# Scan steps of a hybrid token mixer: reordered operations, running maxima computed ahead, and context tiles summed in one state

## What is computed

```python
# SSD, chunks of 128 tokens, per head: a = dt * A
states = einsum('bcqgn,bgrcq,bcqgrp->bcgrpn', Bc, exp(a_cum[..., -1:] - a_cum), xc)
y_diag = einsum('bcqgn,bcsgn,bgrcqs,bcsgrp->bcqgrp', Cc, Bc, exp(segsum(ac)), xc)
y_off = einsum('bcqgn,bcgrpn,bgrcq->bcqgrp', Cc, start_states, exp(a_cum))
# mLSTM, chunks of 128 tokens, per head: b = cumsum(logf)
g = b_last[..., None] - b + ic
m_loc = max(g, axis=-1)
w = exp(g - m_loc[..., None])
C_loc = einsum('bhcs,bcshd,bcshe->bchde', w, vc, kc)
def step(carry, inp):
    C, n, m = carry
    Cl, nl, ml, bl = inp
    m_new = maximum(bl + m, ml)
    C_new = exp(bl + m - m_new) * C + exp(ml - m_new) * Cl
    return (C_new, n_new, m_new), (C, n, m)
# then, with m0 the m before the chunk
m_t = maximum(b + m0, max(Dm, axis=-1)); s = (q @ k.T) * exp(Dm - m_t)
num = s @ v + (q @ C0) * exp(b + m0 - m_t); h = num / max(|den|, exp(-m_t))
```

## Time and profile before

| | |
|---|---|
| median of 3 runs | 3796.38 us (3788.16 to 3798.47) |
| profiled execution, its own time | 3790.32 us |
| its span | 3788.5 us |
| busy: TensorE, VectorE, ScalarE | 3603.6 (95%), 2733.1 (72%), 2024.5 us (53%) |
| attention, layer 0 and layer 1 | 250.0 to 292.1 and 2649.0 to 2672.0 us |
| scan on VectorE, layer 0 and layer 1 | 292.8 to 435.1 and 2672.9 to 2751.9 us |

### The profile page before, as it was taken

How to read it: one execution, slowest core, us unless ns; L and a number is a source line. 1 busy time by engine, 2 the same in 40 slices (tenths; PEclk the granted TensorE clock), 3 DMA queues, 4 the chain that set the end, 5 groups by cost and what they waited for, 6 DMA issues and landing times.

```text
span 3788.5 us, 61038 instructions
## 1 busy us (share of the span) xinstructions
PE 3603.6 (95%) x22630; PEld 3150.5 (83%) x22630; DVE 2733.1 (72%) x5634; ACT 2024.5 (53%) x4207; POOL 0.2 (0%) x4
## 2 busy tenths in 40 slices
PE   7999999999998999999999999989899999979998
PEld 5887787788887899999997888868698888868887
DVE  4556744499969688888768766674765899687666
ACT  3353522466668555555557544444454666684443
POOL 0000000000000000000000000000000000000000
PEclk9998899999999999999999999999999999999999
DMA  5213222356554566665665566533044565605665
GB/s 201 85 61 110 86 96 99 112 179 186 183 161 145 161 185 187 184 186 184 185 187 152 160 188 189 182 118 111 1 151 134 175 187 182 186 22 158 190 190 161
DMA packets 142198, 568.34 MB, mean 150 GB/s; under 512 B 15808, under 2 KB 17344, under 8 KB 130240
## 3 DMA queue, kind: packets, MB, share of 16 engines
q1 hardware_dynamic: 142016, 566.16, 47.5%
HBM read 565.05 MB, written 1.05 MB: 149 GB/s over the span
## 4 chain that ended last, share of the span: by engine, by line
PE 78%; DVE 17%; ACT 3%; issue 1%; DMA 0%; SPq 0%; DVEq 0%; ACTq 0%
PE ps L538 48%; PE ps L964 12%; PE ps L982 10%; DVE arena L1651 8%; PE ps L966 6%; DVE low L1651 3%; ACT arena L1133 2%; DVE hot_found L1651 1%; DVE arena L2143 1%; DVE arena L2134 0%; DVE ring_low L1651 0%; DVE arena L2136 0%; DVE arena L2131 0%; DVE arena L2140 0%; PE ps L752 0%
## 5 line engine op out<-in xcount | busy, mean ns | idle before, releaser
L1133 ACT ACTIVATE high<-ring 128x512 fp32r<-128x512 f32 x1632 | 1028.3, 632 | 1019.2 <-PE ps L538 499.1
L1651 DVE TENSOR_TENSOR low<-ring,high 128x512 fp32r<-128x512 f32 x1632 | 1075.5, 688 | 288.6 <-ACT high L1133 278.0
L538 PE MATMUL ps<-h_pair,high 128*128 128x512 f32 x3456 | 1234.7, 397 | 17.3 <-DVE h_pair L1651 10.1
L538 PE MATMUL ps<-h_pair,low 128*128 128x256 f32 x3456 | 978.6, 283 | 0.0
L538 PEld LDWEIGHTS ps<-h_pair,high 128*128 128x128 f32 x3456 | 652.5, 189 | 170.6 <-issue 11.9
L964 PE MATMUL ps<-wt,high 128*128 128x512 f32 x2048 | 713.2, 394 | 5.7 <-DVE low L1651 5.7
L538 PEld LDWEIGHTS ps<-h_pair,low 128*128 128x128 f32 x3456 | 653.8, 189 | 0.0
L966 PE MATMUL ps<-wt,low 128*128 128x256 f32 x2048 | 572.0, 279 | 0.0
L1133 ACT ACTIVATE arena<-ps 128x256 f32<-128x256 f32 (+2 forms) x658 | 273.3, 425 | 395.7 <-PE ps L538 348.1
L964 PEld LDWEIGHTS ps<-wt,high 128*128 128x128 f32 x2048 | 385.1, 188 | 93.0 <-issue 3.0
L538 PE MATMUL ps<-arena 128*128 128x128 f32 (+7 forms) x2536 | 373.2, 321 | 92.1 <-ACT arena L1133 64.4
(11 more groups left out here) (177 smaller groups left out, 4090.7 us busy)
## 6 DMA issues: line engine op xcount, KB each, us to landing
ring<-u_in SPq DMA_DIRECT2D x384, 512.0 KB, 3.6
ring<-v_in SPq DMA_DIRECT2D x384, 512.0 KB, 3.6
ring<-win_in SPq DMA_DIRECT2D x56, 1024.0 KB, 4.8
ring<-wmod_in SPq DMA_DIRECT2D x24, 1024.0 KB, 5.1
ring<-wq_in SPq DMA_DIRECT2D x48, 512.0 KB, 3.6
ring<-wmod_in SPq DMA_DIRECT2D x48, 512.0 KB, 3.8
ring<-wbr_in SPq DMA_DIRECT2D x16, 768.0 KB, 4.3
ring<-wout_in SPq DMA_DIRECT2D x8, 1024.0 KB, 4.9
```

The lines of the kernel that those rows point to most:

```text
L538: return pe.matmul(o, l_, r, start=first, stop=last)
L1133: return act.activation(o, i_, f, **kw_)
L1651: return dve.tensor_tensor(o, a, b, op)
```

## The change

It does four things. (1) In both layers the running maxima of all steps (`m_at`, `m_max`) and the weights `ap_` and `wk` (`carry`) are made at once, amid attention: two small matmuls turn `rr` and spread its maxima, VectorE runs `chain()` at entry 1, ScalarE one Exp. The steps then only read them. (2) In layer 0 the three blocks of rows of a step come from turned columns (`row_T`, made amid attention) with 32 rows of the array each, the three interleaved; the rows of a step stand ahead of its C·B products in both layers. (3) Within a step, VectorE makes `cb` and `xc` behind the small vectors and `rW` ahead of `ssd_m`; TensorE has the second modulation row and `ml_wT` ahead of `ssd_y`; `ml_num` is read ahead of `ml_dst`. (4) In layer 1 the two context steps of each direction are gone; `context_weights`, `context_states` and `context_read` make their summed state amid attention (entries 3 to 11), the decay of the first tile through the second folded into its weights.

```diff
+                pe.wait_ge(*at("decays", "cm", l))
+                b = claim("cums", "turn", l)
+                mm(b[0:32, 0:P], rr.rearrange("p a b -> p (a b)"), ident).then_inc(*inc("cums", "turn", l))
                 token_slot(s0 + SLOT_MV[1], "mv", 1, list(range(NT)))
+                b = claim("cums", "max", l)
+                pe.wait_ge(*at("decays", "diag", l))
+                mm(b[:, 0:32], ones[0:32, :], top_diag).then_inc(*inc("cums", "max", l))
...
+                def context_states(d):
...
+                    pe.wait_ge(*at("ml_kw", l, d, 1))
+                    pe.wait_ge(*at("ssd_xd", l, d, 1))
...
+                        for n in range(2):
+                            i = mm(b[gp, 0:256], B_tm[:, ORDER[d][n], gp], xd_ctx[n][:, g * 256:(g + 1) * 256],
+                                   n == 0, n == 1)
...
+                            for n in range(2):
+                                i = mm(b[:, (h % 2) * 129:(h % 2) * 129 + 129], kw_ctx[n][:, h * P:(h + 1) * P],
+                                       mv[:, ORDER[d][n], h, :], n == 0, n == 1)
...
+                    if s_ in (4, 8) and unshown(l):
+                        context_states(s_ // 4 - 1)
+                    if s_ == 8 and l == 0:
+                        b = claim("att_o", "rows", l)
...
+                            i = mm(b[0:96, n * P:(n + 1) * P], row_cols[:, n, :], ident)
...
-                    for n, t in enumerate(ORDER[d]):
+                    for n in range(unshown(l), NT):
...
+                        for j in range(4):
+                            for r_ in parts:
...
+                                if l == 0:
+                                    i = mm(b[r_][:, j * P:(j + 1) * P], ident[rows, c:c + 1].broadcast_to([32, P]),
+                                           row_T[rows, tc])
+                                else:
+                                    col = rr[:, t, c - 64:c - 63] if r_ == 2 else cm[:, t, c - 32 * r_:c - 32 * r_ + 1]
+                                    i = mm(b[r_][:, j * P:(j + 1) * P], col.broadcast_to([P, P]), ident)
...
+                            rest_of_mod(MOD_FIRST + 2 * (d * NT + n) + 1)
+                            b = claim("ml_wT", l, d, t)
...
                             b = claim("ssd_y", l, d, t)
...
+                def chain():
...
+                    for n in range(NT - 1):
+                        for d in range(2):
+                            i = tt(m_max[:, 3 * d + n, :], row_max[:, 2 * ORDER[d][n] + d, :], m_at[:, 4 * d + n, :], ALU.max)
+                        link(i)
+                        for d in range(2):
+                            i = tt(m_at[:, 4 * d + n + 1, :], m_max[:, 3 * d + n, :],
+                                   cums[:, 2, ORDER[d][n], 16 + 4 * d:20 + 4 * d], ALU.add)
+                        link(i)
...
+                    if s_ == 1:
+                        chain()
+                    if s_ in (7, 11) and unshown(l):
+                        context_read(s_ // 4 - 1)
+                    if s_ in (3, 7) and unshown(l):
+                        context_weights(s_ // 4)
...
-                        if kept_on:
-                            i = dve.tensor_reduce(mloc, rows, AX.X, ALU.max)
...
-                        if kept_on:
-                            link(tt(mmax, mloc, m_now, ALU.max))
-                            tt(ap_, m_now, mmax, ALU.subtract)
-                            tt(wk, rr[:, t, rc], mmax, ALU.subtract).then_inc(*inc("ml_g", l, d, n))
-                            dve.wait_ge(*at("ml_g", l, d, n))
-                            link(tt(m_now, mmax, cums[:, 2, t, fc], ALU.add))
```

More of the change, by code:

```diff
@@ L334, in cols, with unshown, state @@
             return 0 if l < DEPTH - 1 else SEQ
+        def unshown(l):
+            return NT - len(outs(l))
+        def state(l, d, n):
+            if n == unshown(l) - 1 and d:
+                return last_st, last_cst
+            return st[:, n % 2, :], cst[:, n % 2]
         def passes(l):
@@ L757, in values @@
                     if part == 0:
+                        if unshown(l) and t != outs(l)[0]:
+                            pinned.discard(cnt.now["bank", "att_o", (l, t - 1)])
                         out_bank[t] = claim("att_o", l, t)
@@ L768, in values @@
                     i.then_inc(*inc("att_pv", l, t, part))
-                    if part:
+                    if part and not unshown(l):
                         pinned.discard(cnt.now["bank", "att_o", (l, t)])
@@ L1373, in _ @@
                         copy_p(*att[s_ + 1])
+                    if s_ == 2:
+                        act.wait_ge(*at("decays", "chain", l))
+                        fn(carry_all, carry_all, ACT.Exp).then_inc(*inc("ssd_exp", "carry", l))
+                    if s_ == 10 and l == 0:
+                        act.wait_ge(*at("cums", "rows", l))
+                        fn(row_T[0:96, :], ps[cnt.bank("att_o", "rows", l)][0:96, :], ACT.Copy
+                           ).then_inc(*inc("att_o_read", "rows", l))
                     if h == HEADS[2] and t != outs(l)[0]:
@@ new lines, in context_read @@
+                def context_read(d):
+                    s_to, c_to = state(l, d, 1)
+                    dve.tensor_copy(s_to, bank("ssd_dst", l, d, 1)[:, 0:256]).then_inc(*inc("ssd_dst_read", l, d, 1))
+                    for hp in range(2):
+                        b = bank("ml_dst", l, d, 1, hp)
+                        dve.tensor_copy(c_to[:, 2 * hp:2 * hp + 2, :], b[:, 0:258].rearrange("p (a b) -> p a b", a=2)
+                                        ).then_inc(*inc("ml_dst_read", l, d, 1, hp))
+                    dve.wait_ge(*at("ml_dst_read", l, d, 1, 1))
@@ L1850, in _ @@
                         divide(s_ + 3, *att[s_ + 3])
+                    if s_ == 1:
[4 more added lines that the diff above has]
+                        context_weights(s_ // 4)
+                    if s_ == 3 and l == 0:
+                        link(dve.memset(row_cols, 0.0))
+                        for r_ in range(2):
+                            dve.tensor_copy(row_cols[:, :, 32 * r_:32 * r_ + 16], cm[:, :, 0:16])
+                        dve.tensor_copy(row_cols[:, :, 64:72], rr).then_inc(*inc("decays", "rows", l))
                 dve.wait_ge(*at("ssd_exp", "etot", l))
```

199 lines of the change are left out of this document (132 added, 67 removed).

## The result

The changed kernel takes 3759.15 us, the median of four runs (3756.49 to 3759.37); the kernel before, beside it, 3794.87 (four runs, 3788.16 to 3798.47). The ratio is 0.9912, with an interval of 0.9897 to 0.9927. So it is faster by 35.7 us. Repeated later, the ratio was 0.9913 (0.9894 to 0.9932). The profiled execution took 3759.37 us (span 3757.6), against 3790.32 before: 31.0 us less.

What follows compares the result with a forecast made beforehand. Layer 0's scan was taken as bound by VectorE and TensorE waiting on each other while TensorE's clock halves. Scans -31.3 and -18.0, attentions +8.7 and +18.1, sum -22.5; 3796.4 less that, rounded 3774 us, range 3752 to 3796.

Steps and rivals of the forecast that it cites:

- the first rival: Both attentions cover most of the additions and the scan's first steps keep the clock: 3755 us; chance 0.22.
- The ring: Layer 0's middle scan steps: VectorE makes TensorE wait, TensorE's clock halves, VectorE waits 5.36 us for the slow half.
- The middle step, 13.6: Layer 0's scan: a middle step falls from 20.4 us to VectorE's queue of 13.6, with the clock staying up.
- I expect the clock to fall once per direction, 3.3 us each: 6.6: Layer 0's scan: TensorE stands some 2 us between `ssd_dst` and `ml_wT` in each direction's first step, costing 6.6 us.
- Last steps 11.3, hardly less: Layer 0's scan: the last step of each direction takes 11.3 us, against 11.6 before.
- The rows' bound: Layer 0's scan: cheaper rows book no gain of their own; at 2.94 us they would make TensorE the bound, 6 us.
- ScalarE's 3.4 us behind them delay `ml_w`: Layer 1's scan: rows still use all 128 array rows, so ScalarE's work behind them delays `ml_w` by lengthening latent steps.
- The wait for `cm`: Both attentions: turning the maxima makes TensorE wait for `cm`, adding 1.3 us in layer 0 and 1.1 in layer 1.
- what is queued behind counts more than the work: Layer 1's attention: `context_states` holds up later scores, so VectorE waits some 4 us, then some 2.5; 17 more with additions.
- Attention covers more: TensorE's idle pieces in attention stay short and its clock up, so additions cost only VectorE's work: 3755 us; chance 0.22.
- The clock still falls in every step: Layer 0's scan: three small TensorE idles act as one, six steps take 18 us, total 3794; chance 0.17.
- Attention stays at 1.2 GHz: Both attentions: the clock falls behind `chain()` and `context_states` and stays down, 3817 us, slower than before; chance 0.09.

Runs made afterwards that it cites:

- `order_alone`: The kernel before with only the new order inside a step; maxima, full-cost rows and layer 1's context steps stay as before. 3762.47 us, ratio 0.9926.
- `order_undone`: The change with `ml_wT`, the second modulation row and `rW` (and ScalarE's work on that row) back in their old places, both layers. 3767.57 us, ratio 0.9937.
- `rows_full`: The change with layer 0's rows made over all 128 array rows as in layer 1, without `row_T`, its columns and copy. 3757.26 us, ratio 0.9911.
- `states_later`: The change with layer 1's `context_states` one pair of entries later on TensorE, behind the scores. 3753.91 us, ratio 0.9911.
- `chain_early`: The change with the maxima matmul between the halves of the second mv projection and `chain()` right behind it. 3746.64 us, ratio 0.9896.
- `layer1_old_order`: The change with the old order inside layer 1's steps; layer 0 keeps the new one. 3745.41 us, ratio 0.9898.
- `all_three`: The change with layer 1's old step order, early `chain()`, later `context_states`, and `row_T`'s columns right behind `chain()`. 3750.53 us, ratio 0.9892.
- `change_again`: The change, unchanged, run and traced a second time. 3757.13 us, ratio 0.9913.

## Why the prediction was right, point by point

The forecast was 3774, faster; measured 3759, within the range. The change of -22.5 was too small: the stages show -38.5, the medians -35.7. The measured time is 15 us from the forecast and 4 from the first rival, so the number is right in direction and range and not in size; the terms below say where. (The text gives the changed part as "3 to 4% of the span"; its four stages are 286 of 3788 us, 7.6%. No number came from that share.)

**Layer 0's scan**, forecast 31.3 less, measured 40.4. The ring is shown: `order_alone` breaks it, and `order_undone` brings it back in four of six steps. The middle step, 13.6, measured 13.7 and 14.0; the rows, 1.2, measured 1.17. Too dear were three terms. "I expect the clock to fall once per direction, 3.3 us each: 6.6": it fell once, after a wait of 1.04 us in direction 1's first step, and cost 1.5; that step took 13.1. The very first step, 14.6 with ScalarE's share, took 12.3, with VectorE's wait for ScalarE at 1.28. "Last steps 11.3, hardly less": 10.5, because in the scan before they held a wait of VectorE for TensorE (1.20 and 1.44 us), which I had left in. Those are 6.6, 2.3 and 1.5 of the 9.2 that were missing, less 1.1 for direction 1's middle steps and its first.

**The rows' bound.** I booked nothing for the saved TensorE time beyond keeping under VectorE's 13.6, with 6 us as the price of full rows. `rows_full` gives 7.4. The size was right, the path was not mine: in the middle steps it goes over ScalarE. The two outer values of the prediction for TensorE's saving, 14 us and nothing, are both off.

**Layer 1's scan**, forecast 18 less, measured 24.8. Steps of 15.0, 11.3, 13.8 and 12.8 (by reciprocals, and 1.4 behind the last) against 17.5, 12.5, 15.5, 12.5 and 3 for the clock. The step that failed is "ScalarE's 3.4 us behind them delay `ml_w`": they delay it by 1.01, as `cb` and `xc` now lie in between. At full clock (`states_later`) the scan takes 50.3 us where I had 58, so the steps themselves were 7.7 too dear; the 3 us for the clock were near the 3.9 that it cost. What I did not see is that the new order itself costs layer 1 1.0 us and opens the waits in which the clock falls.

**Layer 0's attention**, forecast 8.7 more, measured 10.0. By the experiments: `chain()` and its clock 5.4 (I had 3.0 and 3.4), the columns and `row_T` 4.2 (I had 1.0). I had left out what stands behind the columns: four matmuls (1.11 us), ScalarE's copy, and a second fall of the clock at 271 us. The wait for `cm` was put at 1.3; entry 4 came 1.8 later behind the copy of `cums`. These make 11.4, 1.4 more than was measured; I take that they overlap.

**Layer 1's attention**, forecast 18.1 more, measured 16.7: VectorE's additions 10.2 us (chain 2.8, weights twice 2.5, reads twice 1.2; I had 10.7), waits 1.55 and 4.05 (I had 4 and 2.5, so the larger one came second). The wait for `cm` was put at 1.1; entry 4 came 1.3 later behind the copy of `cums`. `states_later` shows that my reading of the waits, "what is queued behind counts more than the work", was only half right: with the scores ahead, most of the wait moved and did not go.

**The rivals.** *Attention covers more* was nearest in the total, but not in its mechanism: the clock fell in both attentions. Its other half, first steps that keep the clock, came out in layer 0's direction 0; in its direction 1 the clock fell. *The clock still falls in every step* and *Attention stays at 1.2 GHz* did not come: in attention it fell for 3 to 7 us at a time and came back amid `turn_p` and `values`. By the page "TensorE: Matmul & The Clock Gate" of the Trainium skill, Part 4, transposes don't count as busy for the clock in the way that matmuls do. The prediction has half of attention's work as transposes and lets the trace disagree. That was read wrongly: they take 14.1 of TensorE's 38.2 busy us in layer 0 before, and 15.4 of 44.2 in the change. In the change's fall from 257.3 to 264.1 us they are 1.9 of 6.0 busy us. So the traces show that the clock comes back amid this mix, and nothing on transposes alone.

## What to carry to other kernels

Before you remove work from a loop of several engines, look at TensorE's waits: in layer 0 the order of a few groups in its queue and in VectorE's gave 28 us, and all the work removed or made cheaper on top gave 2, since most of it came back in another stage. An order that closes a gap because other work (the modulation row) fills it opens one where that work is missing (here 1.0 us, and 3.9 more where the clock fell), so give each stage its own. Before you credit an edit with a few microseconds, compare the clock of the two stretches: here the same scan differed by 4 us with it. Work moved ahead belongs in a wait of its engine that is there already; put amid a stage that both engines fill, `chain()` with its 2.8 us cost 5.4 in layer 0 and 2.7 in layer 1.

## What the runs showed of the hardware that I had not expected

**No length of wait decides alone whether the clock falls.** I had read the border between 0.92 and 1.56 us. The trace before already spoke against a border: in layer 1's scan the clock held after 1.40 us (at 2675.80) and fell after 1.39 (at 2680.37). It fell after waits of 0.89 (layer 0's attention of the change) and 1.04 us, and held after the same 0.89 in `chain_early`, and through 1.50 (last step of `layer1_old_order`), 2.26 and 2.49 us (`states_later`). After 2.27 us in the change, with the same instructions around it as in `states_later`, it fell; after the wait of 1.50 it fell in `all_three`. Falls were more frequent behind longer waits. In the attentions and scans of all fourteen traces, with the clock at 1.00 before, a fall came with 58 of the 86 waits of TensorE from 1.3 us on, and with 23 of the 131 from 0.7 to 1.3 (in the wait or within 2.4 us behind it). It isn't blind chance from execution to execution either: the seven falls of the change came in the same places in `change_again`. What else decides isn't shown.

**One loop, two periods.** The expert lookup, bound by TensorE (no idle in 240 us, clock 1.00), took 2.773 or 2.827 us a round in each layer of each of the fourteen traces, never anything between, with code, order and granted clock alike; a layer's stretch is some 7 us longer with the second. Before had 2.77 in both layers twice; the change 2.83 in layer 1 once and 2.77 once; `rows_full` and `all_three` 2.83 in both. Nothing in the profile says what sets it. It explains why the profiled executions differ by 31 us and the stages by 38.5. It may make up to 14 us of the spread of a kernel's runs; as only one run of each has a trace, that isn't shown.
